# A two-block network on one core: the start addresses of the stream and of the weight slabs in SBUF

## The reference

```python
# first block
h = rmsnorm(x);  z = h @ w_in                       # 1024 x 2560
y_a = a_bg * dwconv3(a_cg * a_h)
y_b = silu(layernorm(dwconv31(b_val * sigmoid(b_gate)) + b))
x = x + concat(y_a, y_b) @ w_out
h = rmsnorm(x)
x = x + (silu(dwconv3(h @ w_gate)) * (h @ w_up)) @ w_down    # d_ff 2816
x = rmsnorm(x)
# second block, layer 0: pooling mixer; layer 1: attention over a window of 128
h = rmsnorm(x) * (1 + scale) + shift                # shift, scale, gate from c
u, z = split(h @ a_w_in)
x = x + gate * (((pool(u) @ w_group) * a_scale * silu(z)) @ a_w_out)
k, v = kv of the modulated norm of x                # 2 heads of 64, shared
q, z = split(h @ b_w_in)                            # 16 heads of 64
x = x + gate * ((softmax(q k + bias, sink) v * silu(z)) @ b_w_out)
return rmsnorm(x)
```

## The kernel before

| tensor | before | its start mod 64, mod 256 | after | mod 64, mod 256 |
|---|---|---|---|---|
| stream | 3744 | 32, 160 | 3392 | 0, 64 |
| norm_hi | 36512 | 32, 160 | 36160 | 0, 64 |
| norm_lo | 69280 | 32, 160 | 68928 | 0, 64 |
| w_hi0 | 102048 | 32, 160 | 101760 | 0, 128 |
| w_lo0 | 126624 | 32, 160 | 126528 | 0, 64 |
| w_raw0 | 151200 | 32, 160 | 151104 | 0, 64 |
| mix_y_hi0, ffn_y_hi, pooled_hi, q_then_o | 159392 | 32, 160 | 159296 | 0, 64 |

## Time and profile before

### The profile page before, as it was taken

How to read it: one execution, slowest core, us unless ns; L and a number is a source line. 1 busy time by engine, 2 the same in 40 slices (tenths; PEclk the granted TensorE clock), 3 DMA queues, 4 the chain that set the end, 5 groups by cost and what they waited for, 6 DMA issues and landing times.

```text
span 2097.8 us, 24769 instructions
## 1 busy us (share of the span) xinstructions
PE 2068.7 (99%) x9344; PEld 1697.4 (81%) x9344; DVE 1229.8 (59%) x1698; ACT 651.2 (31%) x1089; POOL 751.2 (36%) x441
## 2 busy tenths in 40 slices
PE   8999999999999999999999999999999999999998
PEld 7888888888888888888878888888888878778786
DVE  7999777555654556545675453453562570796555
ACT  7323345121221212212263122122122261675112
POOL 5555626222221222212274122122131461564623
PEclk9999999999999999999999999999999999999999
DMA  4231112332132331323111121111111120010202
GB/s 150 75 111 41 41 51 90 121 110 104 46 120 100 110 104 46 120 100 110 31 41 61 39 62 41 41 60 40 40 61 41 41 71 30 21 41 21 70 11 80
DMA packets 44749, 141.24 MB, mean 67 GB/s; under 512 B 5617, under 2 KB 9857, under 8 KB 44673
## 3 DMA queue, kind: packets, MB, share of 16 engines
q1 hardware_dynamic: 31632, 100.68, 15.0%
q10 hardware_dynamic: 13040, 39.54, 5.2%
HBM read 135.98 MB, written 7.36 MB: 68 GB/s over the span
## 4 chain that ended last, share of the span: by engine, by line
PE 82%; DVE 12%; POOL 2%; ACT 2%; issue 1%; DMA 0%; SPq 0%; POOLq 0%; ACTq 0%; DVEq 0%
PE psum L592 25%; PE psum L593 25%; PE psum L594 25%; DVE psum L1636 7%; POOL temp L443 2%; PE psum L930 1%; PE psum L941 1%; DVE psum L1496 1%; DVE norm_lo L1509 1%; PE psum L659 1%; PE psum L661 1%; PE psum L660 1%; PE psum L909 1%; PE psum L606 0%; ACT norm_hi L1114 0%
## 5 line engine op out<-in xcount | busy, mean ns | idle before, releaser
L408 POOL TENSOR_TENSOR w_lo<-w_raw,w_hi 128x1024 fp32r<-128x1024 f32 x174 | 442.1, 2558 | 973.0 <-ACT w_hi L1034 971.6
L592 PE MATMUL psum<-norm_hi,w_hi 128*128 128x512 f32 x1632 | 637.3, 391 | 3.5 <-ACT temp L1102 3.5
L593 PE MATMUL psum<-norm_lo,w_hi 128*128 128x512 f32 x1632 | 635.9, 390 | 0.0
L594 PE MATMUL psum<-norm_hi,w_lo 128*128 128x512 f32 x1632 | 635.9, 390 | 0.0
L592 PEld LDWEIGHTS psum<-norm_hi,w_hi 128*128 128x128 f32 x1632 | 307.0, 188 | 68.5 <-ACT temp L1102 4.0
L594 PEld LDWEIGHTS psum<-norm_hi,w_lo 128*128 128x128 f32 x1632 | 306.9, 188 | 63.8
L593 PEld LDWEIGHTS psum<-norm_lo,w_hi 128*128 128x128 f32 x1632 | 306.9, 188 | 63.7 <-issue 0.2
L1102 ACT ACTIVATE temp<-psum 128x512 f32<-128x512 f32 x160 | 93.8, 597 | 420.2 <-PE psum L594 395.1
L1559 DVE SCALAR_TENSOR_TENSOR stream<-psum,mods,stream 128x512 f32<-128x512 f32 x160 | 119.3, 750 | 159.2 <-PE psum L594 159.2
L1034 ACT CAST w_hi<-w_raw 128x1024 fp32r<-128x1024 f32 x158 | 159.0, 1048 | 129.0 <-PE psum L594 79.6
L1557 DVE TENSOR_TENSOR stream<-psum,stream 128x512 f32<-128x512 f32 x176 | 118.6, 689 | 83.8 <-PE psum L594 83.6
(11 more groups left out here) (213 smaller groups left out, 2979.3 us busy)
## 6 DMA issues: line engine op xcount, KB each, us to landing
w_raw<-in_slabs SPq DMA_DIRECT2D x175, 512.0 KB, 3.6
ada_raw<-in_ada ACTq DMA_DIRECT2D x10, 3072.0 KB, 12.8
stream<-in_x SPq DMA_DIRECT2D x8, 512.0 KB, 9.3
out<-stream SPq DMA_DIRECT2D x8, 512.0 KB, 2.8
skew_scratch<-row_scratch ACTq DMA_DIRECT2D x1, 3072.0 KB, 17.7
ada_raw<-in_ada ACTq DMA_DIRECT2D x1, 2048.0 KB, 7.8
bias<-skew_scratch ACTq DMA_DIRECT2D x4, 512.0 KB, 4.2
c_act<-in_c ACTq DMA_DIRECT2D x1, 512.0 KB, 9.7
```

Source lines behind the costliest of these rows:

```text
L408: nc.gpsimd.tensor_tensor(WL[place][:, :], RAW[at % 2][:, :], WH[place][:, :].bitcast(f32), ALU.subtract).then_inc(slab_ready, 1)
L592: nc.tensor.matmul(dst, wh, xh, start=n == 0, stop=False)
L593: nc.tensor.matmul(dst, wh, xl, start=False, stop=False)
L594: last = nc.tensor.matmul(dst, wl, xh, start=False, stop=n == len(terms) - 1)
```

## The change

It removes the unused tensor lead_in, so that the stream and the normed stream start 352 bytes earlier, and puts an unused tensor of 16 numbers (64 bytes) ahead of the high slabs and one of 48 numbers (192 bytes) ahead of the low slabs. After it, the large tensors start at multiples of 64; the high slabs start 64 bytes, the low slabs and all that follows 256 bytes further than the normed stream, counted within a 4096-byte row. Later tensors move 96 bytes towards the start. The instructions of all engines, their order and their waits are the same.

```diff
         gain_sq = sb(root, "fin1_gain_squared", [P, KT])
 
-        sb(root, "lead_in", [P, 88])
         X = sb(root, "stream", [P, KT, S])
         HH = sb(root, "norm_hi", [P, KT, S], f32r)
         HL = sb(root, "norm_lo", [P, KT, S], f32r)
+        sb(root, "gap_hi", [P, 16])
         WH = [sb(root, f"w_hi{n}", [P, 1024], f32r) for n in range(6)]
+        sb(root, "gap_lo", [P, 48])
         WL = [sb(root, f"w_lo{n}", [P, 1024], f32r) for n in range(6)]
         RAW = [sb(root, f"w_raw{n}", [P, 1024]) for n in range(2)]
```

## The result

The changed kernel takes 2140.62 us (median of 4 runs, 2139.4 to 2146.5) where the kernel before takes 2098.65 us (4 runs, 2097.45 to 2100.42): ratio 1.0206, 95% interval 1.0194 to 1.0218. It is 42 us slower. The forecast of no change was wrong, and the time lies outside the range. Of the rivals, the one that came nearest is "a distance that is not zero makes load and stream collide", at its price for the high slabs alone (2138 us).

What follows compares the result with a forecast made beforehand. The prediction took the pace of TensorE's matmuls to bound the kernel. Its three terms were all 0, added to 2099.53 us for the profiled execution; forecast 2099.4 us (own range 2095 to 2104), full range 2015 to 2125 us.

Steps and rivals of the forecast that it cites:

- What bounds the kernel: Whole kernel: TensorE busy 2068.7 of 2097.8 us, so only the matmuls' start-to-start pitch, 226.6 ns, matters to first order.
- load and stream out of step: Sign in the changed profile: near 2150 matmuls per unbroken 500 us, against 2208 if nothing changed.
- Step 1: Operands starting at multiples of 64 instead of 32 past one: taken as 0, at most 13.3 ns saved per matmul.
- Step 2: Weights 64 or 256 bytes past the stream: taken as 0, bounds 13.3 ns down and 6.7 ns up per matmul.
- If the two reads collided, a matmul without a load beside it should be shorter.: Matmul at 600.79 streams alone yet takes 0.39 us like its neighbours, so a load costs a stream under 10 ns.
- The distance already changes in the kernel before.: Weight slices step by 512 bytes, streams by 4096, yet the pitch is steady; only distances under 512 bytes untested.
- The Trainium skill's rule: TensorE has independent read ports for moving operand and weight loads and waits for no one: gaps worth 0 us.
- step 3: Residues of other engines' operands: neighbours cost TensorE nothing, pitch 226.5 and 226.6 ns at different loads; taken as nothing.
- The slower rival: Nonzero distance makes loads and streams collide: 2118 us low slabs, 2138 high, 2157 both; chance 0.22.
- The prediction's own sign for it: In the changed profile, a pitch after a wait that no longer differs from the steady one means distance matters.
- The faster rivals: Matmul surplus depends on addresses: all goes, 1984 us, chance 0.10; part goes, 2022 to 2095 us, chance 0.24.
- 13.3 ns "of addresses": Each 512-column matmul's pitch of 226.6 ns over its columns' 213.3 ns, 115 us in all, possibly dependent on operand addresses.

Runs made afterwards that it cites:

- level_0: Kernel before with the lead-in removed and no gaps, so streams and weights stay level at 64 of 256: 2098.96 us, ratio 0.9999.
- level_32: Kernel before with a first pad of 32 bytes and no gaps, all level at 96 of 256: 2102.35 us, one run.
- level_64: Kernel before with a first pad of 64 bytes and no gaps, all level at 128 of 256: 2101.38 us, one run.
- low_64_off: Kernel before, normed stream at its old residue, high slabs level with it, low slabs and gated results 64 bytes further: 2126.67 us, ratio 1.0136.
- gaps_on_old_start: Kernel before with the change's gaps of 64 and 192 bytes, but a 96-byte lead-in keeping the stream's old residue: 2139.6 us, ratio 1.02.
- one_weight_column: Layout of the kernel before; every weight load in lines 592 to 594 reads its first column 128 times, streams untouched: 2127.46 us.
- low_256_off: Kernel before, high slabs level with the normed stream at its old residue, low slabs and gated results 256 bytes further: 2098.46 us, ratio 1.0002.
- one_stream_column: Layout of the kernel before; every matmul in lines 592 to 594 streams its first column 512 times, weight loads untouched: 2025.02 us.

## Why the prediction was wrong

**What bounds the kernel** was right, and so was the measure. The time followed the count of matmuls in 500 us: about 2150 was announced for load and stream out of step, 2144 came. The change of the span (47.0) is nearly that of TensorE's busy time (49.1).

**Step 1, the start of the operands: right.** level_0, level_32 and level_64 keep 226.7 ns, so the one reader for which the trace had no test, the moving operand, does not pay for its start either. Its two tested readers are as before. Line 1637 of the changed kernel by itself, and its transposes in order of time (start and duration in us), which answer to the earlier trace rows:

```profile
L1637 DVE SCALAR_TENSOR_TENSOR psum<-glu,vec,psum x116: 1289/1290/1291, 61.7 to 224.7; 128x1024 f32<-128x1024 f32 x116
```

```profile
1852.20 1.03 PE L942 MATMUL psum<-ident,probs 128*128 128x128 f32 x8
```

The 110 ns was read from one group of eight; over all 240 transposes of the kernel before, 206 of the 208 gaps within a group are 108 to 110 ns, so they don't depend on the start. That 106.7 ns is the full rate of a weight load, which the prediction takes for granted, no row shows.

**Step 2, the distance: this is the step that failed.** Its term for weights 64 or 256 bytes past the stream was 0. The 64 bytes of the high slabs cost 6.7 ns on nearly every matmul, 42 us in all; only the 256 of the low slabs cost nothing. Each of its two reasons was blind to that.

- *"If the two reads collided, a matmul without a load beside it should be shorter."* The one looked at was 0.39 us, as long as its neighbours. But that was in the level layout, in which a load costs its neighbour nothing: a null result at one setting was used for another. Nor would the changed kernel have given it away. Its matmuls in order of time (start, duration, us):

```profile
412.31 0.39 PE L594 MATMUL psum<-ffn_y_lo,w_hi 128*128 128x512 f32 x1
...
412.54 0.40 PE L595 MATMUL psum<-ffn_y_hi,w_lo 128*128 128x512 f32 x1
412.76 0.19 PEld L593 LDWEIGHTS psum<-ffn_y_hi,w_hi 128*128 128x128 f32 x1 [0.26 <-DVE stream L1558]
412.77 0.49 PE L593 MATMUL psum<-ffn_y_hi,w_hi 128*128 128x512 f32 x1
```

  The stream at 412.54 has no load beside it until the next matmul is due (0.23 us on), and it is among the long ones. The effect outlasts the load: low_64_off puts more of it on the stream that follows (9.1 ns from start to start) than on the one beside (2.5 ns), and of its 21 streams with no load beside them 17 take 397 ns, where before 29 of 31 take 388 or 389.
- *"The distance already changes in the kernel before."* It does, in steps of 512 and 4096 bytes, and the cost repeats every 256. All of these steps are the same distance, zero. The text saw the gap ("only distances under 512 bytes are untested") and then took nothing all the same; the changes to be judged were 64 and 256 bytes, both below every step in the trace.

**The Trainium skill's rule** (SBUF — State Buffer, "Who interferes with whom"), two independent read ports for TensorE that wait for no one, was counted in favour of 0 us for the gaps. For the time of a matmul the runs contradict "independent": with the same instructions and neighbours, the distance between weights and stream moves the pitch from 226.7 to 233.3 ns (gaps_on_old_start), and a change of the weight reads alone moves it to 231.6 (one_weight_column). The measurement decides. By what path one read slows the other, the ports or something behind them, isn't shown. That TensorE waits for no other engine agrees with step 3.

**The slower rival** had the cause, a distance that is not zero, and the right row for its size: the 233 ns after a wait is the steady pitch now. The prediction's own sign for it came too: the pitch after a wait no longer differs from the steady one. A collision as the mechanism isn't shown. Its 38 us for the high slabs are close to the measured 42 by luck: it charged two matmuls of three with 6.7 ns each, but all three pay (396, 394 and 396 ns; the gaps behind them 7.3, 4.7 and 8.0 ns longer), and what keeps the total under 57.5 us is, in the profiled execution, mostly shorter waits and fewer matmuls at the low clock. Its 19 us for low slabs at 256 bytes were wrong, since these cost nothing (low_256_off, ratio 1.0002). Where the forecast went wrong with it was the chance: 0.22, of which the dearer half was left outside a range that stopped at 2125 (half of 0.22 is 0.11; the prediction wrote 0.09). With a bound of +6.7 ns on every matmul written down in step 2 (58 us), the range had to reach 2157, since nothing tested had excluded it.

**The faster rivals** stood on 13.3 ns "of addresses". one_stream_column shows that 10.8 of them are indeed how the stream is read, but not one layout tried gives any back. They cost 0.34 of the chances.

**Step 3, the neighbours: right.** The pitch after is 233.5 ns beside a VectorE that is 97% busy and 233.4 beside one at 45%.

## What to carry to other kernels

Where float32r matmuls follow each other without a break, let the weights and the moving operand start at the same residue of 256 bytes; a pad of 256 was free, and where the whole starts made no difference at four starts. Judge such a change by the count of matmuls in a long unbroken stretch, since 3% of pitch hides in rows that are rounded to 10 ns. Before a cost is put at nothing because the trace already holds such steps, ask whether its steps are as fine as the one that is made, or all multiples of one period; and a test for a collision is worth nothing in a layout that may be the one without it.

## What was unexpected of the hardware

- Distance between weights and stream: 226.7 ns at 0 and 256 bytes and mostly at -16, 228.9 at -64 and +192, 231.0 where only the low slabs are at +64, 233.3 at +16, +32, +64 and most others, 234.3 at +96. It shows on the streams; the loads mostly keep 187 or 188 ns (many have 192 at +16).
- The level layout too starts at 233 ns after a wait and comes down to 226.7 with the seventh gap or so; the changed kernel stays near 233.
- Weights that stand still are slower (231.6 ns) than weights that walk level with the stream (226.7).
- A stream on one column runs at 215.8 ns, a walking one at 226.7, one that changes halves every 64 bytes, in its reads and its writes, at 239.9.
- One layout can have two steady rhythms, 231.0 and 233.3 ns (gaps_on_old_start), the faster one held for a whole norm stretch of 177 us.

Open stays by what mechanism the distance stretches a stream that has no load beside it, why one product off costs 13 ns per three and two or three off 20, why the level layout settles after a wait and the other doesn't, why +16 and -16 differ, what the 10.8 ns of the walk are, and what picks the rhythm. The runs show where these effects appear and at which distance; an explanation of the memory behind them would be a guess.
